# The second attention of a two-block kernel, scheduled by pairs of heads: score steps of 64 rows put together by two, three groups for two heads in place of six

## The reference

```
h = rms_norm(x, norm_g)
q, k, v, z = split(h @ w_in, 4)               # w_in 1024 x 8192
q = rms_norm(q per head and map) * 1/8        # 16 heads, 2 maps m of 64 each
k = rms_norm(k per head and map)
for blk in 4 query blocks of 128:             # keys up to the end of the block
    scores[h, m] = q[h, m] @ k[h, m]^T        # contraction over 64
    probs = softmax(scores + alibi bias, causal)
    weights = probs[m = 0] - lam * probs[m = 1]
    o[h] = weights @ v[h]                     # v of 128 columns per head
o = rms_norm(o, head_norm_g) * 0.8
o = o * silu(z)
out = x + o @ w_out                           # w_out 2048 x 1024
```

## Time and profile before

| | |
|---|---|
| median of the runs | 1293.38 us |
| profiled execution, its own time | 1294.7 us |
| its span, first to last instruction | 1293.0 us |
| PE busy | 1283.3 us, 99% |
| DVE busy | 794.8 us, 61% |
| ACT busy | 612.0 us, 47% |
| POOL busy | 305.0 us, 24% |
| granted PE clock | full in every slice (mean 1.000) |

### The profile page before, as it was taken

How to read it: one execution, slowest core, us unless ns; L and a number is a source line. 1 busy time by engine, 2 the same in 40 slices (tenths; PEclk the granted TensorE clock), 3 DMA queues, 4 the chain that set the end, 5 groups by cost and what they waited for, 6 DMA issues and landing times.

```text
span 1293.0 us, 18343 instructions
## 1 busy us (share of the span) xinstructions
PE 1283.3 (99%) x7158; PEld 1081.7 (84%) x7158; DVE 794.8 (61%) x1577; ACT 612.0 (47%) x1300; POOL 305.0 (24%) x203
## 2 busy tenths in 40 slices
PE   8999999999999999999999999999999999999999
PEld 6777888888899999998888887888888888887787
DVE  5435665333479888887334647576767666677743
ACT  4436654333445444445234446455556555656631
POOL 2022310000055656640002402122222213131110
PEclk9999999999999999999999999999999999999999
DMA  6322232333533334233235222222222222223511
GB/s 232 107 58 74 58 98 66 98 98 98 202 125 110 99 119 131 68 130 114 82 116 211 98 90 74 66 74 82 84 96 75 74 74 74 76 72 123 185 59 66
DMA packets 110297, 130.35 MB, mean 101 GB/s; under 512 B 7553, under 2 KB 87425, under 8 KB 110210
## 3 DMA queue, kind: packets, MB, share of 16 engines
q1 hardware_dynamic: 104450, 112.39, 27.0%
q10 hardware_dynamic: 5760, 16.78, 3.5%
HBM read 119.72 MB, written 9.44 MB: 100 GB/s over the span
## 4 chain that ended last, share of the span: by engine, by line
PE 95%; DVE 3%; DMA 1%; issue 1%; ACT 0%; POOL 0%; ACTq 0%; SPq 0%; DVEq 0%
PE ps L869 17%; PE ps L871 16%; PE ps L870 16%; PE ps L874 7%; PE ps L875 7%; PE ps L876 7%; PE ps L1093 4%; PE ps L1096 4%; PE ps L1095 4%; PE ps L1151 3%; PE ps L1161 1%; DVE wlo L1534 1%; PE ps L1133 1%; PE ps L1185 1%; PE ps L1175 1%; PE ps L1176 1%
## 5 line engine op out<-in xcount | busy, mean ns | idle before, releaser
L1534 DVE TENSOR_TENSOR wlo<-raw,whi 128x512 fp32r<-128x512 f32 (+1 forms) x294 | 239.8, 842 | 173.7 <-ACT whi L1215 172.8
L1215 ACT ACTIVATE whi<-raw 128x512 fp32r<-128x512 f32 (+2 forms) x338 | 208.7, 650 | 115.6 <-PE ps L871 90.1
L869 PE MATMUL ps<-whi,hth 128*128 128x512 f32 x592 | 244.2, 413 | 0.2 <-DVE wlo L1534 0.2
L871 PE MATMUL ps<-wlo,hth 128*128 128x512 f32 x592 | 231.8, 392 | 0.0
L870 PE MATMUL ps<-whi,htl 128*128 128x512 f32 x592 | 231.2, 391 | 0.0
L1959 POOL TENSOR_TENSOR wlo<-raw,whi 128x384 fp32r<-128x384 f32 (+1 forms) x44 | 48.9, 1129 | 416.8 <-ACT whi L1215 416.8
L869 PEld LDWEIGHTS ps<-whi,hth 128*128 128x128 f32 x592 | 111.3, 188 | 31.3 <-issue 9.5
L871 PEld LDWEIGHTS ps<-wlo,hth 128*128 128x128 f32 x592 | 111.1, 188 | 25.0
L870 PEld LDWEIGHTS ps<-whi,htl 128*128 128x128 f32 x592 | 111.6, 189 | 18.9
L1484 ACT ACTIVATE px<-px,nm 128x128 f32<-128x128 f32 (+3 forms) x128 | 70.7, 554 | 90.2 <-DVE nm L1872 90.2
L874 PE MATMUL ps<-hth,whi 128*128 128x512 f32 (+1 forms) x288 | 111.9, 389 | 0.0
(11 more groups left out here) (347 smaller groups left out, 2857.6 us busy)
## 6 DMA issues: line engine op xcount, KB each, us to landing
raw<-in_l_w_in SPq DMA_DIRECT2D x64, 512.0 KB, 4.4
raw<-in_w_gate_up SPq DMA_DIRECT2D x44, 512.0 KB, 4.7
raw<-in_w_in SPq DMA_DIRECT2D x13, 1024.0 KB, 5.1
raw<-in_w_down SPq DMA_DIRECT2D x10, 1024.0 KB, 4.9
raw<-in_l_w_out SPq DMA_DIRECT2D x8, 1024.0 KB, 5.1
raw<-in_w_in SPq DMA_DIRECT2D x26, 256.0 KB, 3.3
raw<-in_w_branch SPq DMA_DIRECT2D x8, 512.0 KB, 3.9
raw<-in_w_out SPq DMA_DIRECT2D x4, 1024.0 KB, 5.1
```

Source lines behind the costliest of these rows:

```text
L869: e.matmul(o, ah, wh[:, cs], start=a, stop=False)
L871: m = e.matmul(o, ah, wl[:, cs], start=False, stop=z)
L1215: return e.activation(out, in_, ACT.Copy, **how)
L1534: return e.tensor_tensor(out, src, hi_part.bitcast(F32), ALU.subtract)
```

## The change

```
-            merge(self.proj2(g + 1), 32, self.slots(2 * g, 2 * g + 2), 14)
+            merge(self.proj2(g + 1), 32, self.pair(2 * g), 14)
...
+    def scores(self, h, ev):
+        self.put("s2", h, ev, self.bank(), self.bank())
+
+    def second_tiles(self, h):
+        b = self.bank()
+        if h >= 1:
+            self.put("ga", h - 1, b, 3 * P)
+        self.put("t2", h, 1, b)
+        if h >= 1:
+            self.put("gb", h - 1, b, 3 * P)
+
+    def pair(self, even):
+        put, bank, odd, past = self.put, self.bank, even + 1, even > 0
+        self.scores(even, 0)
+        self.scores(even, 1)
+        yield
+        if past:
+            put("t2", even - 1, 0, bank())
+        put("cb", even, 0)
+        put("ab", odd)
+        yield
+        if past:
+            self.second_tiles(even - 1)
+        put("cb", even, 1)
+        yield
+        if past:
+            put("t2", even - 1, 2, bank())
+        put("cb", even, 2)
+        yield
+        self.scores(even, 2)
+        self.scores(odd, 0)
+        yield
+        if past:
+            put("to", even - 2, bank())
+        put("cb", even, 3)
+        yield
+        if past:
+            put("p2", even - 1, bank())
+        put("cb", odd, 0)
+        if odd + 1 < H2:
+            put("ab", odd + 1)
+        yield
+        put("cb", odd, 1)
+        yield
+        put("t2", even, 0, bank())
+        yield
+        self.second_tiles(even)
+        yield
+        self.scores(odd, 1)
+        self.scores(odd, 2)
+        yield
+        if past:
+            put("to", even - 1, bank())
+        put("t2", even, 2, bank())
+        put("cb", odd, 2)
+        yield
+        put("p2", even, bank())
+        put("cb", odd, 3)
+        yield
+        yield
...
     def last_heads(self):
-        yield from self.slot(14)
-        self.put("xb", (0, 1, 3))
-        last = self.slot(15)
...
+        for i, _ in enumerate(self.pair(14)):
+            if i == 6:
+                put("xb", (0, 1, 3))
+            elif i == 9:
+                put("xb", (2,))
+            yield
+        yield
+        yield
+        put("t2", 15, 0, bank())
...
```

More of the change, by code:

```diff
@@ L501, in proj2 @@
                 yield
[L503 to L512, removed]
-        yield
[L514 to L535, removed]
-        yield
[L537 to L552, removed]
-        yield from self.slot(14)
-        self.put("xb", (0, 1, 3))
-        last = self.slot(15)
[L556 to L560, removed]
+    def scores(self, h, ev):
[7 more added lines that the diff above has]
+            self.put("gb", h - 1, b, 3 * P)
@@ L561, in last_heads @@
         yield
         yield
[L563 to L567, removed]
+    def last_heads(self):
+        put, bank = self.put, self.bank
+        for i, _ in enumerate(self.pair(14)):
[4 more added lines that the diff above has]
+            yield
         yield
         yield
-        self.put("to", 15, self.bank())
+        put("t2", 15, 0, bank())
+        yield
+        self.second_tiles(15)
+        yield
+        yield
+        put("to", 14, bank())
+        put("t2", 15, 2, bank())
+        yield
+        put("p2", 15, bank())
+        yield
+        yield
+        b = bank()
+        put("ga", 15, b, 0)
+        put("gb", 15, b, 0)
+        yield
+        yield
+        put("to", 15, bank())
```

## The result

The changed kernel took 1297.65 us (median of 7 runs, 1295.51 to 1298.56), the kernel before 1293.78 us on the same chip (7 runs, 1293.19 to 1294.63): ratio 1.0028, 95% interval 1.0018 to 1.0037. That is 3.9 us slower and outside of the range of 1287.8 to 1296.0. The profiled execution took 1296.68 us with a span of 1294.9. In it the first score step of this layer started at 766.02, in the one before at 767.03. From there to the end the changed kernel's trace is 2.9 us longer. That is what the traces can account for; 1.0 us of the 3.9 between the medians has no place in them. The runs of the changed kernel differ by 3.1 us among themselves.

What follows compares the result with a forecast made beforehand. PE, busy 99% of the span, was taken to bound the kernel. Removed 7.2 us less 6.25 us of waits gave 0.95 us net off the median of 1293.38: 1292.4 us, 8-in-10 range 1287.8 to 1296.0.

Steps and rivals of the forecast that it cites:

- place 3: Last stage, reloaded weights' split behind added reductions and exponentials: PE waits 0.9 us, ends 0 and 2.
- banks: Double group claims all four free PSUM banks: no cost, at most 0.1 to 0.2 us once.
- Junction: Each of 24 removed changes between 64-row and 128-row matmuls, in and out, saves 0.30 us: 7.2 us.
- D: Rival: a group's second step pays its own way in and out, so nothing is removed: 1299.6 us, chance 4%.
- Place 1: Second q/k transposition (`qt` of token block 1) waits for `qs`: 0.4 us in six stages, 2.4 us.
- C: Rival: Place 1 alone decides, with a mean wait of 1.2 us, not 0.4: 1297.2 us, chance 16%.
- Place 2: `p2` of the even head waits for `ptl`: 0.9 us over five stages, 1.05 for head 12, 1.0 for head 14.

Runs made afterwards that it cites:

- e3: Changed kernel with weight splits up to the sixth stage at items 1 to 4 of each eight, not 1, 2, 4, 5: 1297.08 us.
- e8: Changed kernel with score steps (14, 2) and (15, 0) apart again in the last stage alone: 1294.86 us.
- e11: Changed kernel with the residual loads (`xb`) issued later in the last stage: 1296.68 us.
- e12: Changed kernel with the edits of e3, e4 and e11 together, all stages by pairs: 1290.55 us.
- e4: Changed kernel with `p2` of the even head one segment later in every pair: 1295.39 us.
- e1: Changed kernel with the new pair order in all stages but the last, which keeps the old slots: 1290.17 us.
- e9: e6 with `t2`, `ga` and `gb` written ahead of `cb` in segment 3 of head 14: 1284.89 us.
- e5: e1 with `p2` of the even head one segment later (e4's edit): 1289.46 us.
- e6: e5 with the weight splits up to the sixth stage at items 1 to 4 of each eight (e3's edit): 1286.39 us.
- e10: e9 with score steps (14, 0) and (14, 1) put together in the last stage: 1286.69 us.
- e7: Changed kernel with nine unused 512-column matmuls put into the pause before the third weight group: 1297.76 us.
- e2: Kernel before with the new pair order in the last stage alone (heads 14 and 15): 1301.52 us.

## Why the prediction was wrong

The forecast was 1292.4, a net gain of 0.95, with 6.25 us of waits. The waits measured are 9.6 us (3.7 + 2.1 + 1.5 + 2.3), and the clock comes on top. The prediction called itself wrong above 9, and it is.

What failed is the price of the last stage. The prediction gave it 1.9 us: 1.0 for `p2` of head 14, 0.9 for place 3, and nothing for the banks and the clock. The trace has 4.8 us of waits there and 3.4 of stretched work at half clock. Two of these terms had been put at nothing, the banks by a count made in another kind of stage and the clock without a reason.

- *Junction.* 7.2 forecast, 9.5 measured, mechanism right. I priced the way in by the first start alone and didn't look at the second pair of the group, though the trace of the kernel before had it (1016.07 and 1016.34 with 384 columns, 0.27 in place of 0.17). D is dead: the inner junction is free.
- *Place 1.* 2.4 forecast, 3.7 measured. The late one is `qn_f`, and the queue in front of it is the one described. 0.48 per stage in place of 0.4, and the first stage, which I counted at none, has 0.77. e3 confirms the split in the queue. C had the right side for the wrong reason: its 1297.2 is near the time by luck, since the mean wait of 1.2 us that it rests on was nowhere.
- *Place 2.* Heads 12 and 14: 2.05 forecast, 2.09 measured. The five other stages: 0.9 forecast, none measured. There the wait at `qt` had already let PE fall back. With it gone (e3) they wait 0.52. I added waits of one pair as if they were independent; they are not. The 1.05 in this sum is when `ptl` had to be ready; the third block itself came 1.20 after the start of `p2` (1246.76 to 1247.96), and `ptl` ended 1.11 after it, so the sum was some 0.06 us too strict.
- *Banks, a step that failed.* "No cost; at most 0.1 to 0.2 us once", since the last users are "at least two items back". That was counted in a stage where two or three items lie between segments. In the last stage one or two do, and `to` takes the bank of the double group one segment earlier: 1.37, and 0.17 at the inner junction. e8, e11 and e12 then had it at `to` of head 13 with 1.9 to 2.6.
- *Place 3, the second one.* 0.9 forecast with an end of 2, 2.28 measured. The split of 1209.73 is late by the whole chain from the transfer issued at 1190.27, which landed 4.83 us later and was the late one for `whi` at 1195.12. It was issued 13.9 us into the stage, in the kernel before 11.6 (1192.78), and ACT waited 0.40 for it, where the prediction had buffers free "at most 2 us later, against transfers that land a half ahead". And "the loads of the residual (`xb`) stay behind the same segments" was wrong by one segment. `last_heads` used to put `xb` after the seventh segment had been yielded, so in the eighth, behind the split that the third weight group waits for; the new one puts it ahead of that yield, in front of the split. e11 got 1.1 us of this pause back by moving it, and lost it at `to` of head 13. No run issues the transfer sooner, so what its lateness costs by itself stays open; e8 shows that it doesn't make the pause alone.
- *The clock, the third one.* 3.4 us in the trace, some 2 us of time by e4's two groups of runs, that no step had. All of the prediction's rows are at full clock, and I had read that as a constant.

Behind the last three is one thing that I didn't see. I priced each wait of the last stage by itself, and there the chain through ACT and DVE is the bound, not PE, once the steps come bunched: it runs for 50 us without PE, 34 of them in this stage. So what is taken away at one wait is in large part spent at the next: in the eight kernels with all three pairs or two of them in that stage the waits sum to between 4.4 and 5.9 us and the stage takes 65.6 to 68.9 (the table above). Where the steps are single there is no wait in e1 and e9, and one of 1.4 in e5 and e6, where PE reaches the stage sooner and POOL's product is late; e9 mended that by order alone. So even with single steps this stage has next to nothing to spare. e10 shows it with one group: 0.4 saved, 1.67 lost.

Three things stay open. One is the 1.0 us by which the medians differ more than the traces. The last stage of e4 is 4.9 us longer than before at full clock, where 5.6 us of waits less 0.3 and three junctions make 4.1: 0.8 us, in pieces under 0.13, that I could not place. And what decides whether the clock falls after a pause of 2 us.

## What to carry to other kernels

Putting steps together that change the array's row mode pays about 0.4 us per junction here. But it bunches the work of the engines behind, so here it paid only in stages where these have slack. Price the stage with the densest queue by itself, and sum its waits along one chain, not one by one. An edit that helps in most places is best tried per stage: e1, which leaves the last stage as it was, turned 3.9 us slower into 3.9 faster. And where a wait is removed, look at once at the next place with no slack, since PE reaches it sooner: e3's edit brought 0.6 us on the changed kernel and 3.1 on e5, where the next place had been given slack.

## What the runs showed of the hardware

- A group of 64-row matmuls also pays at its second pair: 0.34 in place of 0.23 us with 512 columns (1015.90, 1016.24), 0.27 in place of 0.17 with 384 (1016.07, 1016.34 in the kernel before). Going from 512 to 128 columns inside a group paid nothing (0.23 from 1016.47 to 1016.70).
- The granted clock fell to half, the 1.2 GHz level, after pauses of PE of 2.17 to 2.64 us, for 3.4 us (e7, e8, e11) or 6.8 us (the changed kernel, e2, e3). It did not after a pause of 2.24 in e4, nor after pauses of 1.93 in e2 and in e12. Waits of up to 1.6 us were not followed by it in any profiled execution. I had taken the clock of a stream that is 99% busy for granted.
- Three DMA issues of 0.33, 0.45 and 0.45 us in ACT's queue stood between `px` at 1207.73 and the split at 1209.07. In these 1.34 us ACT starts nothing and is idle for 0.94, and the issues are not counted as busy; moving them (e11) shortened PE's pause by 1.1 us. In the kernel before, where they stand behind the split, they run beside ACT's work (issues from 1207.82 on, `px` at 1207.81, the split at 1208.44), and no wait of PE followed.
